# Expert layer: rows of V given out unevenly among the rows of U (thirteen a group in groups 1 to 7, six or five in groups 8 to 15, in place of nine)

## What is computed

```python
def token_block(args):
    xb, eb, gb = args                       # 128 tokens, 8 heads x 16 experts, their gates
    a = jnp.einsum('td,ted->te', xb, u_tab[eb])
    hidden = gb.astype(xb.dtype) * jax.nn.gelu(a)
    return jnp.einsum('te,ted->td', hidden, v_tab[eb])
```

## Time and profile before

| | |
|---|---|
| median of 3 runs | 3106.89 us (3106.46 to 3109.78) |
| the profiled execution, its own time | 3108.23 us |
| its span | 3106.4 us |
| expert stage: first dot product on DVE to the end | 1853.64 to 3106.4 us |
| last U row's group over, V rows alone from here | 2760.82 us |
| busy over the span | PE 88%, DVE 68%, ACT 37%, POOL 32% |

### The profile page before, as it was taken

The page is one execution under the profiler, slowest core; times in us unless marked ns, Lnnn a source line. Parts: engine busy times, 40 slices in busy tenths (PEclk is TensorE's granted clock), DMA queues, the critical chain, the costliest instruction groups (busy, mean ns, idle before and its releaser), DMA issues.

```text
span 3106.4 us, 34641 instructions
## 1 busy us (share of the span) xinstructions
PE 2728.9 (88%) x12196; PEld 1978.6 (64%) x12196; DVE 2112.7 (68%) x2869; ACT 1146.9 (37%) x1980; POOL 981.4 (32%) x566
## 2 busy tenths in 40 slices
PE   8999999999999999999999994676667786769997
PEld 8888788888887888999779891222223332235433
DVE  5687665555564555445555679788788887779877
ACT  5455655555553335445665540000002330034000
POOL 0011000000000000000000027877777877778864
PEclk9999999999999999989999997889898988888999
DMA  6444445555555554443345469999999999999997
GB/s 264 148 161 163 175 178 188 187 189 186 190 187 184 189 188 170 163 163 136 136 164 178 162 234 387 414 415 413 409 417 398 418 413 406 407 383 378 406 412 302
DMA packets 123586, 827.89 MB, mean 267 GB/s; under 512 B 22167, under 2 KB 22183, under 8 KB 23855
## 3 DMA queue, kind: packets, MB, share of 16 engines
q0 software_dynamic: 79392, 510.36, 40.6%
q1 hardware_dynamic: 43920, 313.73, 27.8%
q10 hardware_dynamic: 144, 2.10, 0.2%
HBM read 892.00 MB, written 4.22 MB: 289 GB/s over the span
## 4 chain that ended last, share of the span: by engine, by line
PE 18%; POOL 13%; DMA 10%; DVE 9%; issue 4%; ACT 3%; DVEq 0%; ACTq 0%
POOL rows L1289 13%; PE ps L598 12%; DMA rows<-peer_u,arena 6%; DVE arena L2388 3%; DMA rows<-peer_v 2%; PE ps L1196 2%; PE ps L1207 1%; DMA rows<-peer_v,arena 1%; ACT arena L1750 1%; PE ps L1187 1%; DVE arena L209 1%; DVE arena L202 0%; DVE arena L203 0%; DVE arena L206 0%; DVE arena L199 0%
## 5 line engine op out<-in xcount | busy, mean ns | idle before, releaser
L503 DVE SCALAR_TENSOR_TENSOR WL<-ring,PA,WH 128x512 fp32r<-128x512 f32 x896 | 633.6, 753 | 474.4 <-ACT WH L486 458.6
L1207 PE MATMUL ps<-rows,rstd 128*128 128x512 f32 x1164 | 631.6, 696 | 302.5 <-DMA rows<-peer_v,arena 213.4
L2388 DVE CUSTOM_DVE_ANT_0 arena<-rows,arena 128x2048 f32<-128x2048 f32 x256 | 586.9, 2293 | 146.1 <-DMA rows<-peer_u,arena 118.5
L1207 PEld LDWEIGHTS ps<-rows,rstd 128*128 128x128 f32 x1164 | 246.9, 222 | 674.2 <-issue 380.8
L1289 POOL DMA_INDIRECT rows<-peer_v,arena x256 | 491.7, 1921 | 199.5 <-DVE arena L2388 77.2
L485 ACT ACTIVATE WH<-ring,PA 128x512 fp32r<-128x512 f32 x448 | 324.3, 724 | 552.2 <-PE ps L598 405.3
L1289 POOL DMA_INDIRECT rows<-peer_u,arena x256 | 437.6, 1709 | 167.3 <-DVE WL L503 79.8
L598 PE MATMUL ps<-WH,HH 128*128 128x512 f32 x1120 | 442.3, 395 | 4.3 <-DVE WL L503 4.3
L598 PE MATMUL ps<-WH,HL 128*128 128x512 f32 x1120 | 437.6, 391 | 0.0
L598 PE MATMUL ps<-WL,HH 128*128 128x512 f32 x1120 | 437.3, 390 | 0.0
L598 PE MATMUL ps<-HH,WH 128*128 128x256 f32 x1088 | 312.7, 287 | 17.7 <-DVE WL L503 17.7
(11 more groups left out here) (361 smaller groups left out, 3549.7 us busy)
## 6 DMA issues: line engine op xcount, KB each, us to landing
ring<-stream SPq DMA_DIRECT2D x292, 1024.0 KB, 4.8
rows<-peer_v POOLq DMA_DIRECT2D x32, 1024.0 KB, 15.0
rows<-peer_u,arena POOLq DMA_INDIRECT x256, 14.7
rows<-peer_v,arena POOLq DMA_INDIRECT x256, 14.8
arena<-xT SPq DMA_DIRECT2D x4, 512.0 KB, 8.9
bias_rows<-bias_scratch POOLq DMA_DIRECT2D x1, 2048.0 KB, 10.4
arena<-xT ACTq DMA_DIRECT2D x1, 2048.0 KB, 9.7
arena<-memT POOLq DMA_DIRECT2D x1, 2048.0 KB, 9.1
```

Source lines behind the costliest of these rows:

```text
L503: ins = nc.vector.scalar_tensor_tensor(out=half_tile(WL, u)[:, s], in0=raw_half(u)[:, s], scalar=gain[d], in1=half_tile(WH, u).bitcast(f32 ...
L1207: last = mm(ps[:, 4 * tt + q, :], DIAG[:, k % DIAGS, :], rows[:, SLOTS[n % ROWS], q * CH:(q + 1) * CH], start=n == mine[0], stop=n == ends[q])
L2388: ins = V.tensor_tensor_reduce(out=JUNK, in0=rows[:, SLOTS[n % ROWS], :], in1=HN[:, tt, :], scale=1.0, scalar=0.0, op0=ALU.mult, op1=ALU.a ...
```

## The change

The single number 9 becomes a list by group. Its sum is 135 as before, so `N_LEAD`, the number of rows (544), `ROW_LAST` (391) and everything from that row on stay as they are, the ring slots of that part too. What is new is where 28 of the V rows stand.

```diff
-LEAD = 9
+LEADS = [0] + [13] * 7 + [6, 6, 6, 6, 5, 5, 5, 5]
...
-N_LEAD = LEAD * (GROUPS - 1)
+N_LEAD = sum(LEADS)
...
         ROW_ORDER.append(("u", _g, _j))
-        if _g and LEAD * _j // PEER_K != LEAD * (_j + 1) // PEER_K:
+        if LEADS[_g] * _j // PEER_K != LEADS[_g] * (_j + 1) // PEER_K:
             ROW_ORDER.append(("v", *V_ORDER[_v]))
             _v += 1
```

## The result

The changed kernel takes 3111.78 us (median of 20 runs), the kernel before 3106.16 us (20 runs): a ratio of 1.0020, 95% interval 1.0013 to 1.0026. It is slower by some 5.6 us, where 3.5 us less were forecast. Of the trace after, four readings matter. It is of one execution, of 3112.80 us.

A forecast was written before the change was run, and what follows sets the result against it. Transfers were taken as the bound, at 414 GB/s in groups 2 to 8. Terms -2 - 2.5 + 1 + 0 = -3.5 us gave 3103.4 us from 3106.89, with an 8-in-10 range of 3096 to 3117 us.

The forecast's parts named there:

- The transfers' lengths: Group lengths set by transfers: 65.9 us in groups 1 to 7, 52.3 in 8 to 11, 50.2 in 12 to 15; sum 0.
- Rival 3: POOL becomes the bound in the V-dense groups, 67.8 us a group against 65.9: +13, 3120 us; chance 0.08.
- rival 4: PE becomes the bound in groups 1 to 7, with V rows at 6.58 us: +137 us; chance 0.02.
- The signs named beforehand: Signs of error: under 400 GB/s in groups 9 to 14, or groups 2 to 7; part behind row 391 over 2 us different.
- Term a: Group 1: POOL issues one more row while blocked on a slot DVE holds during `choose`; -2 us, bounds -2.5 to 0.
- Term b: Group 9: the second of POOL's two waits for PE, 4.17 us, should go; -2.5 us, bounds -3.3 to 0.
- Term c: Groups 9 to 12: DVE falls 6.1 us behind, the ring of twelve hides about 5.4; +1 us, bounds 0 to +6.1.
- rival 2: DVE becomes the bound in groups 9 to 14, the ring tolerating less lateness: +14.5 less 2, 3119.4 us; chance 0.11.
- The last 153 rows are the same: The rows from row 391 on keep their order, so no change of time was put down for them.
- Term d: POOL's pace of issuing: fewer bytes per issue in V-dense groups, more in later ones, may cancel; 0 us.
- rival 1: Holes in groups 1 and 9 close, groups 13 and 14 reach 414 GB/s: -8.4 us, 3098.5 us; chance 0.27.
- PE's and ACT's covers: Groups 1 to 7: thirteen V rows take PE 56 us of 65.9; ACT's diagonals hidden at 16 to 45% busy.

The follow-up runs named there:

- the pair of kernels above: Thirteen V rows and all chooses in groups 1 to 7, against the kernel before: late groups dense to the end, 3097.72 us; sparse in the last, 3102.01 us.

## Why the prediction was wrong, step by step

- **The transfers' lengths** (groups 1 to 7 at 65.9, rates unchanged): right. Groups 2 to 7 took 396.06/6 = 66.0 us. Rival 3 (POOL) and rival 4 (PE) did not come: POOL kept up at 416 GB/s, and PE's granted clock rose to 0.93.
- **The signs named beforehand:** two of them came, rates under 400 GB/s in groups 13 and 14 (394) and a part behind row 391 that differs by more than 2 us (3.1).
- **Term a, group 1, -2 us:** the mechanism was right to the row. Measured against 414 GB/s, group 1 lost 51.40 x (1 - 365/414) = 6.1 us before and 58.14 x (1 - 377/414) = 5.2 us after: a gain of 0.9 us.
- **Term b, group 9, -2.5 us:** one wait went, as said. The group lost 3.3 us before and 55.04 x (1 - 401/414) = 1.7 us after: a gain of 1.6 us, and of what is left POOL's wait of 2.36 us is DVE's. (The third V row of the group stands at place 10 and not at 11; the term rests on the first two.)
- **Term c, DVE, +1 us: here the main failure lies.** The step as the prediction put it, "it needs (235.51 - 22.5)/4 = 53.3 us a group" and 49.6 us in groups 13 and 14, is mis-sized. A wait's row counts the whole gap before the instruction, the ordinary step that would be there anyway included; so a group's length less its waits comes out too short. That step is 0.15 us: with 16 waits in four groups it makes 53.3 into 53.9, and with 14 in two groups 49.6 into 50.7. Where DVE really never waits it needs 54.5 (group 9, in the kernels with fifteen rows and with five in groups 9 to 12), 53.8, 53.8, 53.8, 51.1 and 50.8 us. Against 52.3, 52.3, 52.3, 50.2, 50.2 and 50.2 it is late by 2.2 + 1.5 + 1.5 + 3.6 + 0.9 + 0.6 = 10.3 us and not by 6.1. It also does not stay level in groups 13 and 14. What the lateness cost is not measured by itself; it is what the two gains leave of the stretch, 1.9 + 0.9 + 1.6 = 4.4 us, where I took +1. So the ring hid 5.9 us of 10.3, and the 5.4 us of the prediction were about right. It is rival 2, at a third of its price: DVE became the bound as it says, but not because the ring tolerates less, and its own additions (a wait per group that is never made up) did not come.
- **"The last 153 rows are the same": the second failure.** I priced the part behind row 391 at nothing because its order is unchanged. It took 3.1 us more. 1.6 of these are the later start of the dense rows, which goes with the slower V row at the handover; that density in the last groups sets this is argued from the pair of kernels above and the table, and not shown with the changed kernel itself. For the other 1.5 us the cause is open. The transfers had 1.5 MB more left to move behind the last group, 3.6 us at 414 GB/s, which may be it; but the traces do not bear out such a rule (the kernel with fifteen rows took 348 us with 127.7 MB left, before 345.6 us with 128.4).
- **Term d, 0 us:** with thirteen rows nothing was seen of POOL's price. What rival 1 hoped for in groups 13 and 14 came only with eleven rows (415 and 410 GB/s), where DVE was not the bound.
- **PE's and ACT's covers** in the stretch: nothing was seen of a price there. (ACT's busy share, put at 16 to 45%, is 6 to 30% in the earlier trace rows.)

Together, in the two traced executions: c +3.4, a +1.1, b +0.9 and the part behind +3.1 over what I had put down, less 0.5 for the earlier start. That is the 8.0 us between -3.5 and the span's +4.5. The medians lie another 1.1 us apart, which these two traces cannot place.

## What to carry to other kernels

When work is moved between stretches that one resource bounds, add up the second engine's need from its instructions at their start-to-start spacing, not from a stretch's length less its waits; then the slack that you hand out is the real one. Spreading one kind of load unevenly paid clearly here only together with the other kind: the dense groups had some 17 us of VectorE's waits each, and moving `choose` there made the same spread some 9 us faster (3.5 us under the kernel before in place of 5.6 over it). With a dense end besides it was the fastest, 7.4 us under before. And a part whose order is unchanged can still change its length with what stands right before it, so it needs a term of its own.

## What the runs showed of the hardware that was not expected

One and the same V row on PE (eight records) took 3.67 us at the handover where PE had idled 1.3 to 3.0 us before it, with a granted clock of 0.89 to 1.00 over the last 30 us of the U rows, and 6.06 to 6.46 us where it had idled 6.28 us or more, with 0.66 to 0.83. In the changed kernel it took 5.39 us after 5.69 us of idleness, with 0.69. With 2.45 to 3.02 us of idleness both 3.67 and 5.2 to 5.37 us were seen. The clock has two levels, 1.2 and 2.4 GHz; over the row itself the granted clock was 1.00 in the first kind and 0.56 to 0.70 in all the others, so these are rows during which it changed. The Trainium skill, page "TensorE: Matmul & The Clock Gate", section "Part 1: The HAM clock gate", says that the clock falls when PE has been idle and that the moment of its change is not tied to the instructions, so that one kernel comes out differently from run to run; the two values at like idleness agree, though no run here repeats one kernel's profile to show it. The part behind row 391 differed by up to 8 us among the thirteen traces; how much of that is this row's and the clock's stays open beyond the few us that the row itself differs by.

POOL's issue took mostly 2.14 us beside DVE's dot products, sometimes up to 3.04 us, and 0.99 us beside `choose`. In the kernel with fifteen rows, groups 10 to 12 had the fewest V rows, DVE never waited, and POOL was busy only 115.22 of 161.30 us: it waited 27.3 us for DVE and 2.0 us for PE. So the transfers fell to 370 GB/s because slots came free at DVE's pace, not because POOL could not issue more.
